# Norm sums one chunk earlier, and the first block weights split earlier, in a four-sublayer decoder step

## The reference

```python
def rms_norm(x, g):
    y = x * lax.rsqrt(jnp.mean(x * x, axis=-1, keepdims=True) + EPS)
    return y * g

def swiglu(h, w_gate, w_up, w_down):
    return (jax.nn.silu(h @ w_gate) * (h @ w_up)) @ w_down

for layer in range(2):
    x = x + 0.5 * swiglu(rms_norm(x, g_ffn1[layer]), ...)   # D 1024, FF 2816
    h = rms_norm(x, g_mix[layer])
    x = x + (mlstm_mixer(h, ...) if layer == 0 else gdn_mixer(h, ...))
    x = x + cross_attend(rms_norm(x, g_xattn[layer]), mem_k, mem_v, w_q, w_o)
    x = x + 0.5 * swiglu(rms_norm(x, g_ffn2[layer]), ...)
y = rms_norm(x, g_final)
```

## Time and profile before

| | |
|---|---|
| median of 3 runs | 2473.24 us |
| lowest, highest | 2471.74, 2481.8 us |
| the profiled execution's own time | 2476.47 us |
| its span, first to last instruction | 2474.7 us |
| PE busy | 2417.9 us, 98% |
| weight loads on PE | 2355.2 us, 95% |
| VectorE busy | 1839.2 us, 74% |
| ScalarE busy | 1190.1 us, 48% |
| POOL busy | 193.8 us, 8% |
| chain that ended last | PE 81%, DVE 10%, ACT 4%, DMA 2% |
| mean granted clock | 0.991 |

### The profile page before, as it was taken

How to read it: one execution, slowest core, us unless ns; L and a number is a source line. 1 busy time by engine, 2 the same in 40 slices (tenths; PEclk the granted TensorE clock), 3 DMA queues, 4 the chain that set the end, 5 groups by cost and what they waited for, 6 DMA issues and landing times.

```text
span 2474.7 us, 48972 instructions
## 1 busy us (share of the span) xinstructions
PE 2417.9 (98%) x20335; PEld 2355.2 (95%) x20335; DVE 1839.2 (74%) x2861; ACT 1190.1 (48%) x1758; POOL 193.8 (8%) x143
## 2 busy tenths in 40 slices
PE   8999999999999999999999999999899999999998
PEld 7999999988998999999999999999889989999998
DVE  7998864335685699885999876778647684899875
ACT  6555532234444555553655643544345353555543
POOL 0000010012110100001000001001111110100001
PEclk9999999999999999999999999999899999999999
DMA  5333325221685343333334333222325593343332
GB/s 140 102 102 107 103 82 130 73 87 46 205 258 193 89 108 102 98 104 94 98 105 110 88 106 100 69 69 70 107 61 154 190 314 111 96 110 108 81 106 70
DMA packets 476920, 281.34 MB, mean 114 GB/s; under 512 B 24939, under 2 KB 465004, under 8 KB 476706
## 3 DMA queue, kind: packets, MB, share of 16 engines
q1 hardware_dynamic: 449720, 230.83, 34.2%
q0 software_dynamic: 8704, 33.56, 3.6%
q10 hardware_dynamic: 18314, 14.45, 1.9%
HBM read 261.31 MB, written 17.69 MB: 113 GB/s over the span
## 4 chain that ended last, share of the span: by engine, by line
PE 81%; DVE 10%; ACT 4%; DMA 2%; issue 2%; POOL 0%; SPq 0%; ACTq 0%; DVEq 0%
PE ACC L1156 9%; PE ACC L1155 9%; PE ACC L1157 9%; PE ACC L495 6%; PE ACC L496 6%; PE ACC L497 6%; PE M L1645 3%; PE M L1647 3%; PE M L1646 3%; PE ACC L1645 2%; PE ACC L1647 2%; PE ACC L1646 2%; PE M L1155 2%; PE M L1156 2%; PE M L1157 2%
## 5 line engine op out<-in xcount | busy, mean ns | idle before, releaser
L495 PE MATMUL ACC<-xg_hi,w_hi 128*128 128x260 f32 x1152 | 331.6, 288 | 3.2 <-DVE tmp L777 2.0
L496 PE MATMUL ACC<-xg_lo,w_hi 128*128 128x260 f32 x1152 | 326.3, 283 | 0.0
L497 PE MATMUL ACC<-xg_hi,w_lo 128*128 128x260 f32 x1152 | 326.1, 283 | 0.0
L1155 PE MATMUL ACC<-T_hi,wq 128*128 128x260 f32 x1120 | 316.3, 282 | 0.0
L1156 PE MATMUL ACC<-T_lo,wq 128*128 128x260 f32 x1120 | 316.2, 282 | 0.0
L1157 PE MATMUL ACC<-T_hi,wq 128*128 128x260 f32 x1120 | 316.0, 282 | 0.0
L586 ACT ACTIVATE w_hi<-raw 128x1024 fp32r<-128x1024 f32 x106 | 112.1, 1057 | 301.5 <-PE ACC L497 297.2
L592 DVE TENSOR_TENSOR w_lo<-raw,w_hi 128x1024 fp32r<-128x1024 f32 x106 | 129.8, 1224 | 151.1 <-ACT w_hi L586 150.4
L1241 ACT ACTIVATE wq<-wS 128x1024 fp32r<-128x1024 f32 x160 | 169.1, 1061 | 129.1 <-PE ACC L1157 66.9
L495 PEld LDWEIGHTS ACC<-xg_hi,w_hi 128*128 128x128 f32 x1152 | 218.0, 189 | 7.9 <-issue 6.1
L496 PEld LDWEIGHTS ACC<-xg_lo,w_hi 128*128 128x128 f32 x1152 | 217.9, 189 | 0.0
(11 more groups left out here) (727 smaller groups left out, 7549.9 us busy)
## 6 DMA issues: line engine op xcount, KB each, us to landing
raw<-in_ffn_w_down SPq DMA_DIRECT2D x64, 704.0 KB, 4.9
wraw<-in_ffn_w_gate SPq DMA_DIRECT2D x80, 512.0 KB, 4.7
wraw<-in_ffn_w_up SPq DMA_DIRECT2D x80, 512.0 KB, 4.8
cache<-in_cache_mem_v POOLq DMA_DIRECT2D x16, 1024.0 KB, 8.1
raw<-in_gd_w_in SPq DMA_DIRECT2D x32, 512.0 KB, 4.1
raw<-in_ml_w_in SPq DMA_DIRECT2D x24, 512.0 KB, 3.9
cache<-in_cache_mem_k POOLq DMA_DIRECT2D x12, 1024.0 KB, 7.5
raw<-in_xa_w_q SPq DMA_DIRECT2D x16, 512.0 KB, 4.5
```

Source lines behind the costliest of these rows:

```text
L495: pe.matmul(out, wh, hi[:, k, m], start=begin, stop=False)
L496: pe.matmul(out, wh, lo[:, k, m], start=False, stop=False)
L497: mm = pe.matmul(out, wl, hi[:, k, m], start=False, stop=end)
L1155: pe.matmul(out, w[:, 0, k], hi, start=k == 0 and name in "152", stop=False, skip_group_check=True)
```

## The change

There are two parts.

The norm's sums (`pe_norm_tok`) move up on PE. In `pe_phase` and in the later gate stages they stand ahead of the last chunk of unit 0, behind the wait for that chunk, and no longer behind it. In the first gate stage they move from the third chunk of unit 2's first half to its first, and the broadcast moves from the third chunk of the second half to the seventh chunk of the first half.

In the first gate stage alone, the weights of block products 1 and 2 are split earlier: ScalarE makes the high part of "12" ahead of `T_hi` 2 and no longer behind it, and VectorE makes the low part of "12" behind block sum 2, ahead of block sum 3, and no longer behind quarter sum "6". No instruction is added or removed.

```diff
--- before.py
+++ after.py
@@ -521,6 +521,8 @@
                         pe_norm_bc(pe, r)
                     if j == 0 and r is not None:
                         pe.wait_ge(xg_ready, KC * r + k + 1)
+                        if k == KC - 1:
+                            pe_norm_tok(pe, r)
                     if (j, k) in at:
                         at[j, k]()
                     if k == 2 and j in low:
@@ -532,8 +534,6 @@
                 if j in before:
                     before[j]()
                 pe_unit(pe, ph, j, 0, extra, not (j == 0 and (r is not None or (0 in mid or (0, 4) in at) and not second)))
-                if j == 0 and r is not None:
-                    pe_norm_tok(pe, r)
             if before or mid or low:
                 assert ph.units == 8
                 for j in range(4):
@@ -1344,9 +1345,9 @@
                         pe.wait_ge(acc_free, t0 + 2)
                     for h in range(2):
                         for k in range(KC):
-                            if first and (j, h, k) == (2, 0, 2):
+                            if first and (j, h, k) == (2, 0, 0):
                                 pe_norm_tok(pe, r)
-                            if (j, h, k) == ((2, 1, 2) if first else (2, 0, 1)):
+                            if (j, h, k) == ((2, 0, 6) if first else (2, 0, 1)):
                                 self.pe_spread(pe, r)
                             mm = self.plain(pe, j, k, h)
                     mm.then_inc(mm_done, 1)
@@ -1374,9 +1375,9 @@
                 act_split(act, ph, 0, 1, 2)
                 act.wait_ge(acc_free, ph.t0 + 1)
                 act.activation(tmp[:, 1, 0:T], tmp[:, 0, 0:T], ACT.Silu).then_inc(silu_done, 1)
+                self.high(act, ph, 2, "12")
                 if first:
                     self.act_t(act, ph, f, 2)
-                self.high(act, ph, 2, "12")
                 self.high(act, ph, 2, "4")
                 self.act_t(act, ph, f, 3)
                 act.wait_ge(acc_free, ph.t0 + 3)
@@ -1415,6 +1416,7 @@
                     dve_split(dve, ph, 0, 1, 2)
                     up(0)
                     self.dve_t(dve, f, 2)
+                    self.low(dve, ph, 2, "12")
                     self.dve_t(dve, f, 3)
                     self.dve_t_low(dve, f, 0)
                     self.dve_t_low(dve, f, 1)
@@ -1425,7 +1427,8 @@
                 self.total(dve, f, 2, "57")
                 gate(1)
                 self.total(dve, f, 2, "6")
-                self.low(dve, ph, 2, "12")
+                if not first:
+                    self.low(dve, ph, 2, "12")
                 self.total(dve, f, 2, "3")
                 self.dve_t_low(dve, f, 2)
                 self.low(dve, ph, 2, "4")
```

## The result

The changed kernel takes 2480.7 us (median of 8 runs, 2475.53 to 2482.49), the kernel before 2473.05 us beside it (8 runs, 2470.91 to 2481.8). The ratio is 1.0022, 95% interval 1.0011 to 1.0032: 5.4 us slower, between 2.7 and 7.9. The two medians by themselves lie 7.65 us apart, near the upper end of that. Forecast were 2478.0 us, 4.8 us slower. In a second measurement (11 runs) it was 2478.88 against 2472.58 us, ratio 1.0024, 1.0015 to 1.0032. The profiled execution of the changed kernel took 2477.71 us, with a span of 2475.9 us.

What follows compares the result with a forecast made beforehand. PE, busy for 98% of the span, was taken as the bound. Terms 1.21 + 1.21 + 1.88 + 0 + 0.14 + 0.4 = 4.84, say 4.8 us, on the median 2473.24 gave 2478.0 us; range 2472 to 2484.

Steps and rivals of the forecast that it cites:

- Unit 0's end sets the norm here, and the change puts the sums ahead of it: Projection at 376 us: the mean queues behind unit 2's weight split, which waits for unit 0; moved sums delay it 1.21 us.
- 376 and 1538 us: 1.21 forecast: Two projections: PE waits 0.36 us for POOL, then 0.85 us of sums delay unit 0's end; cost 1.21 us each.
- 653 us: 1.88 forecast: Projection: sums start no earlier because of POOL; the last chunk waits 0.94 us, then 0.94 us more; cost 1.88 us.
- 1925 us: 0 forecast: Projection: a 1.93 us delay fits into PE's later 1.97 us wait before unit 2; cost 0.
- the cover by the store's wait: At 1925 us VectorE's first scaled result waits for a states store, so PE's 1.97 us wait hides the delay.
- Rival 3: At 1925 us the store's landing shifts with the weights' loads and its cover fails: 1.9 us more, 2479.9 us; 8%.
- The later gate stages: 0, 0.14 and 0 forecast: Gate stages at 843, 1191 and 2117 us: only delay exceeding PE's wait before the broadcast costs: 0, 0.14, 0 us.
- PE has 0.72 us of wait to lose: Gate stage at 843 us: PE comes 0.71 us later, absorbed by its 0.72 us wait before the broadcast; cost 0.
- rival 2: Longer stalls bring the clock down in the projections at 376, 653 and 1538 us: 9.6 us slower, 2482.8 us; 12%.
- The first gate stage: +0.4 forecast: At 29 to 51 us: 1.2 us won before product 5, 1.6 us lost to a clock fall after a 3.4 us stall.
- Rival 1: Earlier sums shorten the norm, waits before the broadcasts (3.7 us) go, with the first stage's 1.2 us: 2468.3 us; 10%.
- Rival 4: Later waits take back the projections' delays too; only +0.4 and 0.14 us stay: 2473.8 us; 8%.

Runs made afterwards that it cites:

- the mean taken first: Changed kernel, but in the four projections VectorE takes the mean ahead of the low part of unit 2's weights: 2472.93 us, ratio 0.9996.
- the mean first with the sums behind: Kernel before, with only the projections' mean ahead of the low part of unit 2's weights on VectorE; measured twice: ratios 1.0004 and 1.0001.
- the runs of the projections alone: Kernel before, with only the four projections' sums moved ahead of unit 0's last chunk: 2480.27 us against 2473.49 us, ratio 1.0022.
- the turned-round kernel: Kernel before with VectorE's mean earlier in projections and later gate stages, sums there a chunk later, projections' broadcast two chunks later: 2471.28 us, ratio 0.9997.
- the last experiment: Kernel before with sums moved ahead of the last chunk in projections and later gate stages, first gate stage unchanged: 2479.24 us, ratio 1.0023.

## Why the prediction was right, and where it was not

**The mechanism held.** "Unit 0's end sets the norm here, and the change puts the sums ahead of it" is what the chain after shows, and the mean taken first removes the waits at the broadcast. Apart from the clock, the sums of the later norms cost time in the projections alone. Part of the cost is not the queue's: 0.4 to 0.55 us at a place stay with the mean first, since PE waits at the sums.

**376 and 1538 us: 1.21 forecast, 1.44 measured.** The parts were right, each a little small. From POOL's end (its last addition began at 373.32 us and took 1.60) to the sums went 0.14 us instead of 0.06. From the sums to the next product 0.91 us instead of 0.85. From the last chunk's start to the high part 1.06 us instead of 0.97; the chunk's first product, which now comes behind the sums, takes 0.37 us and not 0.28, as the product behind the sums did before. The forecast wait before L512, 1.56 us, came out as 1.65.

**653 us: 1.88 forecast, 2.0 measured.** The sums started against POOL's addition as before, and the whole shift came through.

**1925 us: 0 forecast.** This is the step that failed, or half of it: the cover by the store's wait. Against the two profiles of the kernel before the cover holds: the stretch is 0.1 or 0.6 us shorter. Against the three other profiles of unchanged code, where PE does not wait for it, it is 2.0 us longer. Rival 3 asked whether the landing shifts in the changed kernel. Counted from PE's instruction at 1920 us, the store is issued at 2.6 us in every profile. It lands at 14.0 and 14.5 us in the two profiles of the kernel before, at 11.6 us in both of the changed kernel, at 12.7 and 12.5 us in the two of the mean first with the sums behind, and at 10.7, 10.7 and 11.8 us in the other three of unchanged code. Two profiles of one kernel agree within 0.5 us, which speaks for a landing that goes with what a kernel does earlier; the runs, below, say that the cover held in part. Whether it differs between executions of one kernel is open. One kernel's wait was taken for a fixed cover. How much comes through on the mean can be estimated from the runs of the projections alone. They take 6.4 us more than before on the mean (2480.21 against 2473.82 us), where the ratio above gives 5.4; with 2475 us times the mean clock's shortfall taken off each run, 6.0 us, give or take 0.7. Of these 1.44 + 2.0 + 1.44 = 4.9 us are the other three places, so about 1.1 us is left for this one, between 0.4 and 1.8 (0.5 by the ratio).

**The later gate stages: 0, 0.14 and 0 forecast.** Apart from the clock it is 0 at all three, and at 1191 us the 0.1 us seen at first (15.09 against 15.00 us, from 1185 to 1200 us) is taken back by 1209 us. The reason is wider than the forecast's "PE has 0.72 us of wait to lose": VectorE bounds these stages up to the last plain unit, as the turned-round kernel shows. The 1.2 us of half clock at 843 us is rival 2's mechanism in a place that it didn't name.

**The first gate stage: +0.4 forecast, +0.5 measured.** From 26.4 us to product 5 the changed kernel is 1.1 us quicker (23.36 against 24.47 us; forecast 1.2), with 3.54 us of wait where 3.4 was forecast, and the next 5.2 us of PE's work are 1.6 us slower (6.74 against 5.15 us; forecast 1.6). The clock fell as expected, after a longer wait than before.

**The rivals.** Rival 1 needed the mean to run when the sums are there; it doesn't, and made to do so (the mean first) it ends the loss, but the kernel is no faster than before. Rival 2 did not come in the projections: after waits of 0.3 to 0.9 us and then 1.65 us, 5.7 us apart, the clock stayed at 2.4 GHz in all four, in both profiles. The Trainium skill (TensorE: Matmul & The Clock Gate, Part 1, What's actually happening) has the slow clock as the default and activity as what releases it; the fall after 3.54 us of standing agrees, the full speed after these waits shows that not every stall counts. What the prediction set against this rival, that the clock stays up after 2.12 us alone, held in the first profile of before and not in that of the last experiment, where half clock came behind just that wait. So that argument rested on too few places. Rival 4 is refuted: the 263.19 us from 386 to 649 us are as before, so what was lost at 376 us stayed lost.

**The sum.** 1.44 + 2.0 + 1.44 + 1.1 + 0.5 + 1.2 gives 7.7 us if every execution has the half clock of 843 us, 6.5 without; the runs say 5.4 (2.7 to 7.9) and 5.9 (3.7 to 7.9). The forecast's 4.8 lacked the 1.1 us at 1925 us and some 0.6 us in the other terms. That it lies so close to 5.4 is in part luck, since the places add up to more. The forecast also put what runs can tell from no change at 12.4 us; the intervals came out at 2 to 3 us either way.

## What to carry to other kernels

Moving a reduction ahead of the last piece of work before it can pay only if its reader is free to run then: follow the reader's own queue, here the mean behind a weight split that hangs on that very piece. And ask whether its input is there by then: here PE waited for it at all seven later norms. A wait seen in one profile is a cover only if other profiles have it too, above all a wait for a DMA. Where several engines are full, a wait taken away can come back behind a later instruction, as in the gate stages here, and the gain is to be read at the end of the stage, not at the wait.

## What was not expected of the hardware

Places of half clock can repeat: the two profiles of the changed kernel have theirs within 0.2 us of one another, up to 1796 us, though they were taken in different measurements. Those of the mean first with the sums behind agree up to 1609 us, and then one has two stretches that the other lacks. Those of the kernel before differ from the first stretch on (6.8 us from 13.1 us, against 3.4 us from 14.6 us), and most places behind it are not the same. Between kernels that differ by 1 us in one stage they lie elsewhere too, as single stretches of 3.4 us or several in a row, each worth about 1.6 us. Against this the 2.1 us won at three places of the mean-first kernel did not show in its runs' ratio.

In the kernel before the wait of 2.54 us for the store was followed by half clock, and after 1.97 us the clock had stayed up. Windows of the second profile of before, columns as above:

```profile
1929.00:1932.80 3.80, 1.26 (x11) 1.08 (x10) 0.92 (x2) 2.07 (x3) 0.00 (x0) 1.00 1.04 416
1932.90:1936.30 3.40, 3.40 (x17) 3.40 (x17) 3.26 (x8) 1.07 (x3) 0.00 (x0) 0.50 0.43 164
```

The power on POOL (L648) took 1.18 us in the projection at 376 us, where VectorE stood idle meanwhile, and 2.12 us in the gate stage at 843 us, where VectorE was adding. The place is not the cause: in the turned-round kernel, where VectorE makes the low part of a weight (L592) during the power at 376 us, it took 2.09 us there; at 843 us, where VectorE was adding for 0.64 us of it only, it took 1.19 us. Timeline of POOL in the changed kernel, with the last addition ahead of the sums at 376 us:

```profile
373.32 1.60 POOL L644 TENSOR_TENSOR ssq<-ssq,sq 128x520 f32<-128x520 f32 x1 [5.60 <-ACT sq L628]
379.50 1.18 POOL L648 TENSOR_TENSOR rtok<-msq,mhalf 104x5 f32<-104x5 f32 x1 [4.58 <-DVE msq L656]
...
851.35 2.12 POOL L648 TENSOR_TENSOR rtok<-msq,mhalf 104x5 f32<-104x5 f32 x1 [5.91 <-DVE msq L656]
```
